# Receptance tiles in quarters behind the first pair's features, and ScalarE's feature steps held out of the scores' phases

## The reference, cut to what matters

```python
r = (xr @ w_rkv[0])                       # receptance, latent tokens
k = (xk @ w_rkv[1]);  v = (xv @ w_rkv[2])
log_w = -RK_DECAY_SCALE * sigmoid(w0 + tanh(xw @ w1) @ w2)     # per direction
a = sigmoid(a0 + (xa @ a1) @ a2)                               # per direction
kk = k * k_k;  kk = kk / max(sqrt(sum(kk * kk)), 1e-12)        # per head
k_dir = k * (1 + (a - 1) * k_a)
# scan, for both directions:
s = s * w_t - (s @ kk_t) (x) (kk_t * a_t) + v_t (x) k_t;   y_t = s @ r_t
# out: group norm of y, + (r . k_dir . r_k) * v, times a gate, @ w_o
```

## Time and profile before

| | us |
|---|---|
| median of 3 runs | 3087.43 |
| profiled execution, its own time | 3085.09 |
| span of the profiled execution | 3083.5 |
| PE busy | 2859.8 (93%) |
| DVE busy | 1897.7 (62%) |
| ACT busy | 1428.7 (46%) |
| POOL busy | 526.2 (17%) |

### The profile page before, as it was taken

One profiled execution on the slowest core, in us unless ns is written; L12 is line 12 of the kernel. 1 busy time (PEld: TensorE's weight loads), 2 busy tenths in 40 slices (PEclk: granted clock), 3 DMA queues, 4 the chain that ended last, 5 costly groups with the idle time before them and its releaser, 6 DMA issues. The chain is left out here.

```text
span 3083.5 us, 62817 instructions
## 1 busy us (share of the span) xinstructions
PE 2859.8 (93%) x26751; PEld 2331.1 (76%) x26751; DVE 1897.7 (62%) x3016; ACT 1428.7 (46%) x2197; POOL 526.2 (17%) x482
## 2 busy tenths in 40 slices
PE   7899899998899889999889999999989977999999
PEld 2795677777778658887549999999956744678877
DVE  4941565555665257765778888888864256466652
ACT  1212555655554242221347777777734345343231
POOL 1001545545542010000010000000010045100000
PEclk9999999999999999999999999999989988999999
DMA  5553000000000277655249999999922210222222
GB/s 206 193 191 127 23 21 21 21 21 21 3 3 4 82 255 277 267 198 199 87 153 424 367 369 363 369 367 372 366 99 105 87 36 19 89 77 96 96 96 82
DMA packets 73843, 482.11 MB, mean 156 GB/s; under 512 B 11107, under 2 KB 13027, under 8 KB 32144
## 3 DMA queue, kind: packets, MB, share of 16 engines
q1 hardware_dynamic: 59360, 418.48, 36.0%
q0 software_dynamic: 11952, 51.91, 4.6%
q10 hardware_dynamic: 2304, 8.39, 0.7%
HBM read 457.20 MB, written 34.13 MB: 159 GB/s over the span
## 5 line engine op out<-in xcount | busy, mean ns | idle before, releaser
L2360 DVE TENSOR_TENSOR sb_moe_w_lo<-w_ring,sb_moe_w_hi 128x1408 fp32r<-128x1408 f32 (+1 forms) x132 | 255.3, 1934 | 69.9 <-ACT sb_moe_w_hi L2305 68.3
L2208 PE MATMUL ps<-sb_moe_w_hi,sb_x_feat_lo 128*128 128x352 f32 x832 | 273.4, 329 | 5.2 <-DVE sb_moe_w_lo L2360 5.1
L2210 PE MATMUL ps<-sb_moe_w_hi,sb_x_feat_hi 128*128 128x352 f32 x832 | 267.5, 321 | 0.0
L2209 PE MATMUL ps<-sb_moe_w_lo,sb_x_feat_hi 128*128 128x352 f32 x832 | 266.8, 321 | 0.0
L2305 ACT ACTIVATE sb_moe_w_hi<-w_ring 128x2816 fp32r<-128x2816 f32 x80 | 204.3, 2554 | 2.5 <-DMA w_ring<-w_moe_up 1.8
L2208 PE MATMUL ps<-sb_moe_w_hi,sb_hid_feat_lo 128*128 128x256 f32 x572 | 163.2, 285 | 3.9 <-DVE sb_hid_feat_lo L2491 3.9
L2208 PEld LDWEIGHTS ps<-sb_moe_w_hi,sb_x_feat_lo 128*128 128x128 f32 x832 | 156.1, 188 | 11.5 <-issue 10.4
L2210 PE MATMUL ps<-sb_moe_w_hi,sb_hid_feat_hi 128*128 128x256 f32 x572 | 161.8, 283 | 0.0
L2209 PE MATMUL ps<-sb_moe_w_lo,sb_hid_feat_hi 128*128 128x256 f32 x572 | 161.8, 283 | 0.0
L2209 PEld LDWEIGHTS ps<-sb_moe_w_lo,sb_x_feat_hi 128*128 128x128 f32 x832 | 157.0, 189 | 0.0
L2210 PEld LDWEIGHTS ps<-sb_moe_w_hi,sb_x_feat_hi 128*128 128x128 f32 x832 | 156.0, 187 | 0.0
(11 more groups left out here) (540 smaller groups left out, 7751.2 us busy)
## 6 DMA issues: line engine op xcount, KB each, us to landing
w_ring<-w_moe_up SPq DMA_DIRECT2D x67, 1408.0 KB, 8.4
sb_hm<-w_ada SPq DMA_DIRECT2D x48, 1024.0 KB, 7.1
w_ring<-w_ffn SPq DMA_DIRECT2D x22, 1024.0 KB, 4.9
w_ring<-w_up SPq DMA_DIRECT2D x22, 1024.0 KB, 4.8
sb_b_again<-w_moe_up SPq DMA_DIRECT2D x13, 1408.0 KB, 8.6
sb_hm<-w_moe_up SPq DMA_DIRECT2D x13, 1408.0 KB, 8.2
sb_t_again<-w_moe_up SPq DMA_DIRECT2D x13, 1408.0 KB, 7.7
w_ring<-w_moe_down SPq DMA_DIRECT2D x13, 1408.0 KB, 7.3
```

What stands on the lines that cost most here:

```text
L2208: pe.matmul(out, x_lo, w_hi, start=first, stop=False)
L2209: pe.matmul(out, x_hi, w_lo, start=False, stop=False)
L2210: return pe.matmul(out, x_hi, w_hi, start=False, stop=end)
L2360: return V.tensor_tensor(WL[:, s, w], raw[raw_at(c, i)[0]][:, w], WH[:, s, w].bitcast(F32), ALU.subtract)
```

## The change

The first pair's plan: a receptance step is now a quarter of a tile (2 of its 8 products). Five quarters stand ahead of Pw0, one ahead of each of Pw1, Pa0, Pa1 and Pnorm, eight ahead of Pg and seven ahead of Gkds: 24 quarters, six tiles. The tiles are taken in the order `FIRST` (0, 1, 4, 5, 6, 7, 2, 3); j is a tile's place in it. The last two (2 and 3, whose weights lie where quad 1's LK will be) follow within quad 0, one quarter before every second item of the plan, after Pv and Av of the first pair; both use bank 5. The features and bonus due in quad 0 are not issued until these are. The ten products of L559 ahead of the first score are gone. The first score waits for five evictions, the one of quad 1 for all eight.

```diff
@@ -944,6 +944,8 @@
+        FIRST = (0, 1, 4, 5, 6, 7, 2, 3)
@@ -955,7 +957,7 @@
         main = ["Pw0", "Aw0", "-", "Pw1", "Aw1", "Dscan0.0", "Gkq", "Pa0", "Aa0", "Dscan0.1", "Pa1", "Aa1", "Dscan0.2", "Gex0",
                 "Asq", "Dscan1.0", "Pnorm", "Dscan1.1", "Aroot", "Dscan1.2", "Gex1", "Drec0", "Gin1", "Drec1", "Drec2",
                 "Drec3", "Drec4", "Drec5", "Dkkn", "APx0", "APi0", "APx1", "APi1", "AP0", "Gkka", "AP1", "APe", "GA", "Pg",
-                "Ag", "Pv", "Av", "GB", "Akd0", "Akd1", "Ark", "Gkdk", "GK", "GR", "Gkds", "Gcoefin"]
+                "Ag", "GB", "Akd0", "Akd1", "Ark", "Gkdk", "GK", "GR", "Gkds", "Gcoefin", "Pv", "Av"]
@@ -997,11 +999,14 @@
         plan, turn = [], 0
         for x in main:
-            if x in ("Pw0", "Pw1", "Pa0", "Pa1", "Pnorm", "Pg"):
-                for n in range(turn, turn + 1 + (x in ("Pnorm", "Pg"))):
-                    plan.append(("receptance", 0, n))
-                turn = n + 1
-            plan.append(("feature", 0, x))
+            n = {"Pw0": 5, "Pw1": 1, "Pa0": 1, "Pa1": 1, "Pnorm": 1, "Pg": 8, "Gkds": 7}.get(x, 0)
+            plan += [("receptance", 0, divmod(j, 4)) for j in range(turn, turn + n)]
+            turn += n
+            if x[1:2] != "v":
+                plan.append(("feature", 0, x))
+        values = [("feature", 0, x) for x in main if x[1:2] == "v"]
+        spare = [("receptance", 0, divmod(j, 4)) for j in range(turn, 4 * 6)] + values + [
+            ("receptance", 0, divmod(j, 4)) for j in range(4 * 6, 4 * N)]
         for p in range(N):
             rec = [x for q in range(QUADS) for x in quad(QUADS * p + q)]
             cut = main.index("Gin1") + 1
@@ -1022,11 +1027,16 @@
             first, turn, stop = 4, ends[0], len(rec) - 16
             done = [0, 0]
             for i, x in enumerate(rec):
+                if p == 0 and i % 2 == 0 and spare:
+                    plan.append(spare.pop(0))
+                if spare:
+                    plan.append(("rec", *x))
+                    continue
                 for at, (side, lo, hi) in enumerate(((early, first, turn - 8), (after, turn, stop))):
                     due = len(side) * min(max(i - lo, 0), hi - lo) // (hi - lo)
                     if at and done[0] < len(early):
                         continue
-                    while done[at] < len(side) and (done[at] < due and (side[done[at]][2][0] != "G" or i not in quiet)
+                    while done[at] < len(side) and (done[at] < due and (side[done[at]][2][0] not in "GA" or i not in quiet)
                                                     or done[at] and side[done[at]][2] in ("Aw0", "Aw1", "Aa0", "Aa1")
                                                     and side[done[at] - 1][2] == "P" + side[done[at]][2][1:]):
                         plan.append(side[done[at]])
@@ -1113,7 +1123,8 @@
                         sp.dma_start(V2[:, u, :], kv[:, TOK:2 * TOK]).then_inc(s_v[u], 16)
 
                     def r_load(p):
-                        sp.wait_ge(s_rst[p % 4], 16 * (p // 4 + 1))
+                        j = FIRST.index(p)
+                        sp.wait_ge(s_rst[j % 4], 16 * (j // 4 + 1))
                         sp.dma_start(r2[:, p % 2, :], A["r_rows"][p]).then_inc(s_r2[p % 2], 16)
@@ -1314,15 +1325,18 @@
 
                     for kind, p, x in plan:
                         if kind == "receptance":
-                            w = ring.all[:, 2 * KT * P * (x // 2):2 * KT * P * (x // 2 + 1)]
-                            if x % 2 == 0:
-                                pe.wait_ge(s_wr[x // 2], 16)
-                            if x >= 6:
-                                pe.wait_ge(s_re, x - 5)
-                            for k in range(KT):
-                                last = pe.matmul(ps[:, x % 6, :], w[:, (2 * k + x % 2) * P:(2 * k + x % 2 + 1) * P], xr[:, k, :],
+                            j, part = x
+                            m = FIRST[j]
+                            w = ring.all[:, 2 * KT * P * (m // 2):2 * KT * P * (m // 2 + 1)]
+                            if part == 0:
+                                pe.wait_ge(s_wr[m // 2], 16)
+                                if j > 5:
+                                    pe.wait_ge(s_re, j)
+                            for k in range(2 * part, 2 * part + 2):
+                                last = pe.matmul(ps[:, min(j, 5), :], w[:, (2 * k + m % 2) * P:(2 * k + m % 2 + 1) * P], xr[:, k, :],
                                                  start=(k == 0), stop=(k == KT - 1))
-                            last.then_inc(s_r, 1)
+                            if part == 3:
+                                last.then_inc(s_r, 1)
                             continue
                         if kind == "feature":
@@ -1348,11 +1362,10 @@
 
                         if head == "score":
                             if n == 0:
-                                pe.wait_ge(s_re, KT)
-                                if p == 0:
-                                    self.keep_warm(pe, 3, 10)
+                                pe.wait_ge(s_re, 5 if p == 0 else KT)
                                 pe.wait_ge(f_pool.sem, f_pool.at("K", p))
                             if n == CCH:
+                                pe.wait_ge(s_re, KT)
                                 pe.wait_ge(f_pool.sem, f_pool.at("R", p))
@@ -1526,12 +1539,15 @@
 
                     for kind, p, x in plan:
                         if kind == "receptance":
-                            act.wait_ge(s_r, x + 1)
-                            if x >= 4:
-                                act.wait_ge(s_rst[x % 4], 16)
-                            S.activation(RB[:, x % 4, :], ps[:, x % 6, :], ACT.Copy).then_inc(s_re, 1)
-                            act.wait_ge(s_re, x + 1)
-                            act.dma_start(A["r_rows"][x], RB[:, x % 4, :]).then_inc(s_rst[x % 4], 16)
+                            j, part = x
+                            if part < 3:
+                                continue
+                            act.wait_ge(s_r, j + 1)
+                            if j >= 4:
+                                act.wait_ge(s_rst[j % 4], 16)
+                            S.activation(RB[:, j % 4, :], ps[:, min(j, 5), :], ACT.Copy).then_inc(s_re, 1)
+                            act.wait_ge(s_re, j + 1)
+                            act.dma_start(A["r_rows"][FIRST[j]], RB[:, j % 4, :]).then_inc(s_rst[j % 4], 16)
```

## The result

| | before | changed |
|---|---|---|
| median (range, runs), us | 3087.67 (3084.74 to 3090.98, 6) | 3102.22 (3095.66 to 3105.68, 6) |
| ratio, 95% interval | | 1.0045, 1.0034 to 1.0056 |
| profiled execution, its span | 3085.09, 3083.5 | 3103.02, 3101.4 |
| PE busy | 2859.8 | 2861.4 |

The changed kernel is 14.5 us slower. The side (slower) and the block ahead of W4 were forecast, the size was not: 6.5 us, and 3102.2 lies above the range's end of 3101.

The account below looks back on a forecast made before the run. Both stages were taken to go at PE's pace. First pair to level 1 -15.5, its later quads +0.4, six periods +18.6, clock +3 sum to +6.5 us: 3093.9 against the median of 3087.43, range 3083 to 3101.

Parts of the forecast that it names:

- the block ahead of W4: Quad 2, middle periods: held table load and three Exp steps precede W4's eviction; U4 waits 2.6 us, Y4 +3.0.
- The start of the scores: First pair: first score at 296.4 instead of 323.57, 27.2 us earlier, set by PE's own work.
- Quad 0: First pair: tiles 2 and 3 moved in add 13.7 us; level 1 at 321.5 against 337.08, -15.5 us.
- The three waits: New in quad 0: 0.25 us for a tile's eviction, 0.85 for the bonus, 1.05 for ACT's sigmoid before Pw1.
- a wait of trans2: Quad 0: the quarter behind score2 covers trans2's wait for the eviction of trans0, saving 1.0 us.
- Pair 0's later quads: After quad 0 in the first pair: kd steps sooner, value copies later; +0.4 us, bounds -0.5 to +1.
- The periods without the clock: Pairs 1 to 6: waits add 3.1 us per period, bounds 2.2 to 3.8; +18.6 us in six.
- The late values: Middle periods: level 1 still waits 1.15 us, X4.10 +1.4, U6's eviction -0.48, coefficient product -0.67.
- Rival 1: Pairs 1 to 6: the block costs nothing, only the first pair's gain stays; -15 us, 3072; chance 0.10.
- Rival 4: Periods: table load costs twice its 1.28 us in its new place; +14 us, 3101; chance 0.04.
- The clock: Periods: half of the six new 2.6 us waits end in PE's lower clock, about 1 us each; +3 (0 to +7).
- Rival 3: Periods: PE's clock falls in each, at 1.2 us; +10.7 us, 3098; chance 0.16.

Follow-up runs that it names:

- e3: Changed kernel plus two warming products (the filler) ahead of U4 in pairs 1 to 6, inside PE's wait; 3097.81 us, ratio 1.0030.
- e1: Changed kernel without the hold: ACT's steps are again issued at quiet places; 3073.85 us, ratio 0.9956.
- e4: Kernel before with only the first pair's change and its value steps late in pair 0 alone, no hold; 3074.70 us, ratio 0.9961.
- e2: Kernel before with the hold alone: ACT's steps not issued at quiet places; 3117.77 us, ratio 1.0092.
- f2: The kernel of e3 run again, beside the changed kernel on one chip; 3094.59 us, ratio 1.0019.
- f3: Changed kernel with ACT's steps held over W, U and Z items among the scores too; 3080.65 us, ratio 0.9978.

## Why the prediction was right in direction and wrong in size

**The start of the scores: right.** Forecast 296.4, measured 297.08, of which 0.61 is a later start of the whole stage (245.69 against 245.08). K was there at 291.18 + 3.42 = 294.6, 2.5 us before PE wanted it, as worked out.

**Quad 0: the waits right, the rest 1.7 us too small.** The three waits were put at 0.25, 0.85 and 1.05; they are 0.17, 0.88 and 0.99. Less the late start, level 1 came 13.85 earlier instead of 15.5, and two terms made it so. First, the eight quarters take 14.7 us from start to start, not 13.7: one between 64-wide products takes 1.91 (313.54 to 315.45) and not 1.72. The sixteen 64-wide products ahead of it take 0.61 (312.93 to 313.54), where the same sixteen cost 0.47 in a run of their kind (32 take 0.93, 467.13 to 468.06). The trace of before had a row for this that I didn't read: a projection of quad 0 takes 1.48 (335.08 to 336.56) among 64-wide products, against the 1.29 among the tiles. Second, I took off 1.0 for a wait of trans2 that the quarter would cover, but in the trace of before trans2 (327.13) doesn't wait, so there was nothing to save. PE's timeline of the kernel before:

```profile
327.13 0.48 PE L1384 MATMUL ps<-sb_consts,sb_Pi 128*128 128x128 f32 x1
...
335.08 1.56 PE L1258 MATMUL ps<-sb_tw,sb_w_pair 128*128 128x384 f32 x4
336.56 0.68 PE L1404 MATMUL ps<-sb_xs,sb_tb 64*64 64x64 f32 x16
```

What went the other way is the half clock of before, put at 1.1: the scores and transposes of quad 0 took 4.97 there (323.57 to 328.54), and the same products take 3.42 in the changed kernel, so it had cost about 1.5. The Trainium skill says on the page "TensorEngine Tiling (Array Packing)", section "Key Properties", that a change of the tiling mode drains TensorE; it gives no figure. The 0.14 and 0.19 us above are in accord with it; no run here measures the drain by itself.

**Pair 0's later quads: +1.1 instead of +0.4**, just outside the bound of +1. From level 1 to pair 1's coefficient product it is 71.15 us in the changed kernel and 70.07 in the one before.

**The periods without the clock: right, in part by two errors that cancel.** U4's wait was put at 2.6 (measured 2.61), X4.10's wait at 1.4 (1.37), the coefficient product's at none (none); +3.1 per period was forecast, and e3 has 90.15 - 87.03 = +3.12. But Y4 is 3.2 later, not 3.0: from the start of score8 to Y4 it is 9.79 us in the changed kernel (449.60 to 459.39) and 6.56 in the one before (548.80 to 555.36). And the 0.15 that the last level's evictions were to give back didn't come. The late values, put at +0.25, change the period by -0.07 (e1 against e4): the waits at level 1 were put at 1.15, and one of 0.63 is there. Rival 1, the block hidden, is refuted by e2. Rival 4, a doubled table load, is refuted by the row pair 452.83 and 454.12: the Exp step starts 1.29 us after the load does. On this the trace stands with the load's figure, not with the drain that the Trainium skill adds in "ScalarE: Activation LUTs", section "What ACT_TABLE_LOAD costs".

**The clock: the term that failed.** I took half of six waits to end in the lower level, at 1 us each: 3 us. It fell in all six periods, five times for 6.8 us (458.2 to 465.0 is one), which makes the period 2.2 to 2.8 us longer than e3's 90.15, and once for 3.4 us (734.7 to 738.1), which makes it 0.6 longer (90.71). So it is six falls at 2.0 on average and not three at 1, and the whole is the 12 us that the filler took out. The count was wrong against the rows at hand: the clock of before had fallen after 2.46 us of idle time, and the new wait was longer. The price was that of the single fall of the earlier trace rows, of 3.4 us, part of which I let fall into the next wait.

The row from 458 to 459, in PE's second wait of 1.27 us, is not the rule for where the clock drops. Read in steps of 0.1 us, it dropped 0.1 to 1.9 us after U4's start in the 18 falls of the changed kernel, its second profile and e2 (six each), and 13 times before the second wait began (at 734.7, 0.5 us after U4's start at 734.22, for one). So the second wait isn't what brings the fall. Whether it makes it last isn't shown: no run has the one without the other.

The sum, in pairs' length: forecast -15.5 + 0.4 + 18.6 + 3 = +6.5. Measured -13.85 + 1.08 + 18.37 + 11.95 = +17.55, where 18.37 is what is left of e3's +5.60 behind the first two terms (six of its periods give 18.7). Of the 11 us missed 9.0 are the clock, 1.7 quad 0 and 0.7 the later quads, less 0.2. Rival 3 (a fall in each period) had the right count with a chance of 0.16 but, at 1.2 each, too small a price: 2.0 on average. The range left out its far end and ended 1 us too low. The side, slower, had been given 0.48 against 0.42 for no change, so that it came out right says little.

**What stays open.** Why the clock dropped at another moment in each period, although the waits are the same. The moment goes with the length: of the 18 falls the four that came within 0.5 us of U4's start lasted 3.4 us (3.5 by these steps in one), the 14 that came 0.6 us or more after it 6.8. Open too is how much of the 12 us a typical execution has: the medians say 9.5, and with the filler two falls in six were left in one profile and none in the other.

## What to carry to other kernels

A hold that keeps steps back must be checked for where it lets them go: they come out together at the first place that isn't held, and what is short and urgent behind them (here an eviction of 0.28 us) waits for all. When a new wait of PE is longer than one behind which the trace shows the clock fall (here 2.6 us against 2.46), let it fall in every one at the range's end, each at half the time at the lower level. Here that would have been 3.4 / 2 = 1.7 us for each, 10 in six: an estimate from the trace of before, against 12 measured. A long step of an engine that also evicts for PE is worth splitting: cutting a 1.96 us copy in two gave 1.0 us in each period.

## What the runs showed of the hardware

The same wait at the same place once left the clock alone and once lowered it. In the trace of before PE stood 2.11 us for the bonus and the projection behind it took 1.53; in e2, where PE's products in quad 0 are the same in the same order, it reads

```profile
333.85 2.90 PE L1258 MATMUL ps<-sb_tw,sb_w_pair 128*128 128x384 f32 x4 [2.11 <-DVE sb_bon L1601]
```

```profile
334.00:335.00 1.00, 1.00 (x2) 0.66 (x3) 0.26 (x2) 0.00 (x0) 1.00 (x1) 0.50 0.65 46
```

(PE's timeline and a window of e2; the clock was at 0.50 from 333.3 to 336.7, and had been from 326.5 to 329.9). I had read the first as "2.11 us doesn't lower it"; one execution can't say so. Nor did 1.88 us of work in the 2.61 us wait always keep it up (two of six in f2, none of six in e3). Where PE's longest waits in a period were shorter (1.51 in f3, 1.37 in e1), no fall was seen in any of them.
